# A deeper ring for gathered rows, two fused layer norms, and GpSimd only beside additions out of PSUM

## What is computed

```python
h = _layer_norm(x, ln_in_g, ln_in_b)
z = h @ w_in[i]                                   # pool channels | q | k | v
mix = jnp.concatenate([y_pool, y_attn], axis=-1) @ w_o[i]
h = _layer_norm(DEEPNORM_ALPHA * h + mix, ln1_g[i], ln1_b[i])
ffn = _peer(h, peer_wq[i], peer_subkeys[i], peer_u[i], peer_v[i])
gate = jax.nn.sigmoid(h @ ple_gate_w[i] + ple_gate_b[i])
ple = gate * (p[i] @ ple_w[i])
h = _layer_norm(DEEPNORM_ALPHA * h + ffn + ple, ln2_g[i], ln2_b[i])

# _layer_norm: (x - mean) * rsqrt(var + 1e-5) * g + b, over the 1024 of a token
# _peer: queries = h @ wq; 8 heads each pick 16 of 128 x 128 experts by two sub-keys;
#   a = h . u_tab[expert]; out = sum over picks of softmax * gelu(a) * v_tab[expert]
```

## Time and profile before

| what | us |
|---|---|
| median of 3 runs (1389.04 to 1395.43) | 1389.6 |
| the profiled execution, device time | 1386.17 |
| its span, first to last instruction | 1384.4 |
| PE busy with matmuls | 1329.3 |
| DVE busy | 1159.9 |
| ACT busy | 664.1 |
| POOL busy | 565.8 |
| last matmul of the program ends | 1370.65 |

### The profile page before, as it was taken

The page is one execution under the profiler, slowest core; times in us unless marked ns, Lnnn a source line. Parts: engine busy times, 40 slices in busy tenths (PEclk is TensorE's granted clock), DMA queues, the critical chain, the costliest instruction groups (busy, mean ns, idle before and its releaser), DMA issues.

```text
span 1384.4 us, 23354 instructions
## 1 busy us (share of the span) xinstructions
PE 1329.3 (96%) x7689; PEld 718.7 (52%) x7689; DVE 1159.9 (84%) x2380; ACT 664.1 (48%) x912; POOL 565.8 (41%) x352
## 2 busy tenths in 40 slices
PE   5989899999999999999999999999989999999995
PEld 3554455545665666666655555555534444444442
DVE  6663759999975999999859888888888989988877
ACT  4552545636668767666534333333433434333332
POOL 2640234435555333233326555655564433322202
PEclk9999999999999999999999999999999999999998
DMA  7222132234665999999989999999999999999951
GB/s 302 77 76 92 50 127 83 92 106 148 187 188 174 324 348 366 367 356 356 393 321 377 365 356 369 361 378 355 371 334 389 385 392 390 385 382 371 365 191 62
DMA packets 148654, 384.52 MB, mean 278 GB/s; under 512 B 11761, under 2 KB 71409, under 8 KB 146417
## 3 DMA queue, kind: packets, MB, share of 16 engines
q1 hardware_dynamic: 111728, 249.54, 51.1%
q0 software_dynamic: 36864, 134.23, 25.8%
HBM read 340.74 MB, written 42.99 MB: 277 GB/s over the span
## 4 chain that ended last, share of the span: by engine, by line
PE 76%; DVE 8%; DMA 6%; issue 6%; ACT 2%; DVEq 0%; POOL 0%; SPq 0%; ACTq 0%
PE bank L610 33%; PE bank L599 12%; PE bank L601 11%; PE bank L600 11%; DMA ple_sb<-v_rows_dram,expert_id 4%; PE bank L627 2%; DVE cut L1203 2%; DVE ple_gate L1627 2%; PE bank L814 1%; PE bank L816 1%; PE bank L767 1%; DMA raw<-tiles_dram 1%; PE bank L561 1%; DVE ple_gate L1549 1%; DVE hn L1222 1%
## 5 line engine op out<-in xcount | busy, mean ns | idle before, releaser
L610 PE MATMUL bank<-cut,area 128*128 128x512 f16 x2304 | 504.2, 380 | 8.3 <-DVE area L1615 5.1
L599 PE MATMUL bank<-hT,cut 128*128 128x384 f16 (+1 forms) x1232 | 413.5, 336 | 6.0 <-ACT gelu_out L1080 1.7
L600 PE MATMUL bank<-hT,cut 128*128 128x384 f16 (+1 forms) x1232 | 413.4, 336 | 0.0
L601 PE MATMUL bank<-hT,cut 128*128 128x384 f16 (+1 forms) x1232 | 413.4, 336 | 0.0
L610 PEld LDWEIGHTS bank<-cut,area 128*128 128x128 f16 x2304 | 224.9, 98 | 277.6 <-DVE area L1615 4.6
L875 ACT ACTIVATE cut<-raw 128x1024 f16<-128x1024 f32 x242 | 252.1, 1054 | 212.5 <-PE bank L610 134.8
L1203 DVE SCALAR_TENSOR_TENSOR cut<-raw,cut 128x1024 f16<-128x1024 f32 x242 | 298.0, 1232 | 43.7 <-ACT cut L875 42.7
L548 POOL DMA_INDIRECT ple_sb<-u_rows_dram,expert_id x128 | 200.2, 1564 | 251.8 <-DVE dots_now L1531 243.7
L548 POOL DMA_INDIRECT ple_sb<-v_rows_dram,expert_id x128 | 177.6, 1388 | 244.2 <-DVE ple_gate L1627 233.5
L538 POOL TENSOR_TENSOR cut<-raw,cut 128x1024 f16<-128x1024 f32 x56 | 125.8, 2248 | 159.1 <-ACT cut L885 159.1
L1627 DVE SCALAR_TENSOR_TENSOR ple_gate<-ple_sb,sparse_w_now,ple_gate 128x1024 f32<-128x1024 f32 x128 | 163.8, 1280 | 17.6 <-DMA ple_sb<-v_rows_dram,expert_id 14.8
(11 more groups left out here) (146 smaller groups left out, 1117.6 us busy)
## 6 DMA issues: line engine op xcount, KB each, us to landing
raw<-tiles_dram SPq DMA_DIRECT2D x298, 512.0 KB, 6.4
gates_scratch<-area SPq DMA_DIRECT2D x12, 2048.0 KB, 13.3
area<-gates_scratch SPq DMA_DIRECT2D x32, 768.0 KB, 9.7
gelu_scratch<-gelu_out SPq DMA_DIRECT2D x80, 192.0 KB, 4.9
area<-gelu_scratch SPq DMA_DIRECT2D x20, 768.0 KB, 11.3
norm_rows<-norms_dram SPq DMA_DIRECT2D x3, 1024.0 KB, 8.8
hn<-x_dram SPq DMA_DIRECT2D x4, 512.0 KB, 5.0
ple_sb<-u_rows_dram,expert_id POOLq DMA_INDIRECT x128, 8.4
```

The lines of the kernel that those rows point to most:

```text
L599: nc.tensor.matmul(dst, w[0], hT[:, 0, k, 0:width], start=(k == 0), stop=False)
L600: nc.tensor.matmul(dst, w[0], hT[:, 1, k, 0:width], start=False, stop=False)
L601: last = nc.tensor.matmul(dst, w[1], hT[:, 0, k, 0:width], start=False, stop=(k == KD - 1))
L610: mm = nc.tensor.matmul(bank[:, 2 * tt + h, :], lhs(a)[:, tt * P:(tt + 1) * P], cut[:, t.slot, b, h * HALF:(h + 1) * HALF], start=(first a ...
```

## The change

Four things are edited.

1. **Ring of gathered rows.** ROW_RING goes from 4 to 8. Slots 0 to 3 stay on `ple_sb`, slots 4 and 5 are the two rows of `norm_rows`, slots 6 and 7 the last 2048 columns of `area`. Since the norm rows are overwritten, the third load of `norm_rows` moves on SP's queue from behind the first query tiles to behind the last weight tile and the last addition.
2. **Norm behind attention.** `mix_norm` replaces `row_moments` and `layer_norm`: one DVE instruction makes (x - mean) * weight from two SBUF inputs while ACT takes the root; the Newton step is three small instructions behind the reciprocal's one and needs no shift; ACT multiplies with rstd; POOL adds the bias for tiles 0 to 2; for the last tile DVE makes x * rstd + bias in one. ACT takes the root of the last tile ahead of the first `take_ple`.
3. **First query.** It waits for `ple_out` 7, the second for 8.
4. **Final norm.** Tile 3's steps are laid between the last v tiles' steps. PE runs token tile 2 of the last four v tiles one half after the other. ACT centres and scales tiles 0 and 1; POOL multiplies both with the weight and adds tile 0's bias; DVE adds tile 1's bias as its last instruction and norms tile 2 in halves, which are stored one by one.

```diff
-ROW_RING = 4
+ROW_RING = 8
-POOL_ADDS = ((), (0, 1, 2), (0, 1, 2))
+POOL_ADDS = ((), (0, 1, 2))
-        expert_rows = ple_sb[:, :, :].rearrange("p (s a) n -> p s (a n)", s=ROW_RING)
+        expert_rows = [*(ple_sb[:, 2 * s:2 * s + 2, :].rearrange("p a n -> p (a n)") for s in range(4)),
+                       *(norm_rows[:, s, :] for s in range(2)),
+                       *(area[:, AREA - (s + 1) * D:AREA - s * D] for s in range(2))]
...
+            sp.wait_ge(rows_used, 2 * HK)
+            load_norms(2)
...
-            add_b(2)
+            pool.wait_ge(norms_in, 16 * 3)
+            pool.wait_ge(centred, TT * 2)
+            own.link(nc.gpsimd.tensor_tensor(hn[:, 0, :], hn[:, 0, :], norm_rows[:, 0, :], ALU.mult))
+            nc.gpsimd.tensor_tensor(hn[:, 0, :], hn[:, 0, :], norm_rows[:, 1, :], ALU.add).then_inc(pool_final, 1)
+            pool.wait_ge(centred, TT * 2 + 1)
+            nc.gpsimd.tensor_tensor(hn[:, 1, :], hn[:, 1, :], norm_rows[:, 0, :], ALU.mult).then_inc(pool_final, 1)
...
-            pe.wait_ge(ple_out, 8)
+            pe.wait_ge(ple_out, 7)
...
+                    if isinstance(it, int) and it == 0 and j == 1:
+                        pe.wait_ge(ple_out, 8)
...
+            for h in range(2):
+                for i, t in enumerate(last):
+                    for step, (a, b) in enumerate(((0, 0), (0, 1), (1, 0))):
+                        mm = nc.tensor.matmul(bank[:, 2 * (ND - 1) + h, :],
...
+                mm.then_inc(experts_done, 1)
...
+                own.link(nc.vector.bn_aggr(moments[:, t, :], stats[:, t, :]))
+                nc.vector.tensor_scalar(v, moments[:, t, 1:2], EPS / ALPHA ** 2, None, ALU.add).then_inc(stats_done, 1)
+                dve.wait_ge(norms_in, 16 * 2)
+                own.mark(nc.vector.scalar_tensor_tensor(out=hn[:, t, :], in0=hn[:, t, :], scalar=moments[:, t, 0:1],
+                                                        in1=norm_rows[:, 0, :], op0=ALU.subtract, op1=ALU.mult))
+                dve.wait_ge(rstd_done, norm_batch(1, t) + 1)
+                own.link(nc.vector.reciprocal(r, std[:, t:t + 1]))
+                own.link(nc.vector.tensor_scalar(n, r, r, v, ALU.mult, ALU.mult))
+                own.link(nc.vector.tensor_scalar(n, n, -0.5, 1.5, ALU.mult, ALU.add))
+                nc.vector.tensor_scalar(r, r, n, None, ALU.mult).then_inc(shift_done, 1)
```

More of the change, by code:

```diff
@@ L1185, in late, with final_root, final_normal @@
                         weight_high(N_BOTH + 8 * e + v + 2, (v + 2) % RING, T_LATE + 8 * e + v + 2 - RING)
-                    if end and v == 2:
-                        roots(2, 0)
+                    if end and v == 1:
+                        final_root(0)
+            def final_root(i):
+                t = norm_order(2)[i]
+                act.wait_ge(stats_done, norm_batch(2, i) + 1)
+                nc.scalar.activation(std[:, t:t + 1], variance[:, t:t + 1], ACT.Sqrt).then_inc(rstd_done, 1)
+            def final_normal(i):
+                t = norm_order(2)[i]
+                act.wait_ge(shift_done, norm_batch(2, 0) + i)
+                nc.scalar.activation(hn[:, t, :], hn[:, t, :], ACT.Identity, bias=shift[:, t:t + 1],
+                                     scale=rstd[:, t:t + 1]).then_inc(centred, 1)
             with act.Fori(0, N_LATE // 8 - 1) as e:
@@ L1250, in row_moments @@
+                r, n = rstd[:], newton[:]
+                own.link(nc.vector.reciprocal(r, std[:]))
                 own.link(nc.vector.tensor_tensor(n, r, r, ALU.mult))
-                own.link(nc.vector.tensor_tensor(n, n, variance[:, cols], ALU.mult))
+                own.link(nc.vector.tensor_tensor(n, n, variance[:], ALU.mult))
                 own.link(nc.vector.tensor_scalar(n, n, -0.5, 1.5, ALU.mult, ALU.add))
                 own.link(nc.vector.tensor_tensor(r, r, n, ALU.mult))
-                nc.vector.scalar_tensor_tensor(out=shift[:, cols], in0=moments[:, cols, 0], scalar=-1.0, in1=r,
+                nc.vector.scalar_tensor_tensor(out=shift[:], in0=moments[:, :, 0], scalar=-1.0, in1=r,
@@ L1729, in late @@
                         split_lo(t.plus(SPLIT_AHEAD))
-                    if end and v == 2:
-                        final_rows(0)
-                    if end and v == 4:
-                        layer_norm(2, 0)
             before = own.count
```

209 lines of the change are left out of this document (127 added, 82 removed).

## The result

The changed kernel takes 1372.17 us (median, 1371.36 to 1374.49) where the kernel before takes 1390.56 in the same comparison. The ratio is 0.9865, with a 95% interval of 0.9837 to 0.9892: 18.8 us or 1.35% faster. I had predicted 12.0 us less, 1377.6, and a range down to 1372.0. Direction and places were right, the size was not: the gain is half as large again.

What follows compares the result with a forecast made beforehand. PE was taken as the bound, busy 1329.3 of 1384.4 us, with DVE what it waits for in the touched places. Gains of 2.6 + 6.9 + 2.5 = 12.0 us from the 1389.6 median gave 1377.6 us, range 1372.0 to 1385.5.

Steps and rivals of the forecast that it cites:

- the turning in front: Norm behind attention: PE starts turning tile 2 at 159.2 instead of 161.14 us, 1.9 us won.
- Front: Norm behind attention through first query: 2.6 us gained with DVE held by POOL, 3.5 us without.
- The hold: Norm behind attention: POOL's addition holds DVE's next variance step 0.75 us, making a tile's pitch 5.9 us.
- rival (a): Front and end: POOL does not hold these DVE instructions; 15.1 us gained, 1374.5 us; chance 0.14.
- What is late next: Front: last tile's root at 154.7 us delays `take_ple`; PE's second pair begins near 155.5, ends at 159.1.
- Middle: Stretch 920 to 1035 us: eight slots end DVE's waits for gathered rows and PE's idle time, 6.9 us gained.
- End: Final norm and last v tiles: the span's end comes 2.5 us earlier, 4.7 us if small steps aren't held.
- The 1.27 us: Late v tiles: PE's wait for a low part goes once tile 3's norm is spread; PE ends at 1369.3.
- The base: Whole kernel: the 12.0 us sum, made on the 1386.17 us profiled execution, was subtracted from the 1389.6 us median.
- (b): Middle: full DMA engines mean the deeper ring buys nothing; 5.1 us gained, 1384.5 us; chance 0.14.
- (c): Late v tiles: gathers crowd out weight tiles, costing 18 us; 1395.6 us, slower; chance 0.06.
- (d): Front: its gain does not appear or is lost to a later transfer; 9.4 us gained, 1380.2 us; chance 0.08.

Runs made afterwards that it cites:

- before_look: The kernel before the change, unchanged, profiled a second time: 1390.48 us.
- ring8_alone: The kernel before with only eight ring slots and the norm rows' load moved behind the last addition: 1382.28 us, ratio 0.9937.
- before: The kernel before the change, unchanged, in its first profiled execution: 1386.17 us, span 1384.4 us.
- fill_gap: The kernel before plus three unread products on PE, placed one pair too late, behind the idle piece of the norm behind attention: 1392.19 us, ratio 1.0017.
- front_alone: The kernel before with only the new norm behind attention and the first query waiting for seven instead of eight halves: 1383.78 us, ratio 0.9947.
- after_ring4: The changed kernel with the ring back at four slots: 1378.68 us, ratio to the kernel before 0.9907.
- fill_gap_b: The kernel before plus three unread products on PE inside the idle piece of the norm behind attention: 1387.16 us, ratio 0.9966.
- end_alone: The kernel before with only the new final norm: 1386.43 us, ratio 0.9964.

## Why the prediction was right, and where it failed

Places and mechanisms were right, and the size was too small. The terms that failed are those for PE's idle pieces. The first is the turning in front: the 1.9 us priced for it were 3.5 even at full clock. PE turned tile 2 11.98 us behind the last product with w_o before (161.14 less 149.16) and 8.45 us after (158.06 less 149.61). The second was put at nothing: each piece was priced at its idle time, with the clock taken as 1.00 behind it. In `before_look` the 3.4 us in front cost 2.7 us more by the clock, and the timed runs give the front 7.4 us and not 2.6.

**Front: right places, 2.6 us predicted, 4.6 in the first pair, 7.4 alone.** Three steps of it failed.

- *The hold.* I priced the variance step as held by POOL, since an instruction on 128x4 was the earlier trace rows. The row was right and the step from it wrong: on 128x1 there was no hold in front (0.15 us at 153.00) nor for the Newton steps at the end (0.27 at 1360.35). The pass with two SBUF inputs was held, as I said, but for 0.3 to 0.6 us of each tile, not 0.75. So the mechanism lies between my forecast and rival (a), nearer to (a). Its end of 4.7 us fits; its front of 3.5 is below the 4.6 measured, for the next two reasons.
- *What is late next.* I let `take_ple` wait for the last tile's root until 154.7 and PE's second pair begin near 155.5. The root came at 153.19, `take_ple` at 153.29, and the pair at 154.63. From there PE had no gap at all, so the turning was bound by PE's own order: 1.6 us more than priced for the turning, and 0.4 us more behind it.
- *The clock.* I read 1.00 in the earlier trace rows and took the idle piece at its length. The trace of before could not show it there, but it showed the same thing elsewhere: behind the idle piece of 3.03 us that ends at 101.33 its clock is 0.50 from 102 to 106 us. The Trainium skill, page "TensorE: Matmul & The Clock Gate", section "HAM oscillation — how this bites in real kernels", says that idle gaps of PE between bursts bring the lower clock; the second profile of before agrees (0.50 at 162 to 166), the first does not (1.00 there). I should have had it as a rival: the front by 1.7 to 2.7 us more.

**Middle: the mechanism was right, the remainder was not foreseen.** All of the waits for gathered rows went, as the round of slots said. (One sum on the way was wrong: 1 us per pair over 16.7 pairs is 17 us and not 13, so it did not show DVE falling behind; that the rows held PE is shown by `ring8_alone`.) "So all of it goes" was true of them and not of PE: with the rows there in time, PE waits for the next in line, a weight tile near 1025 us (2.6 us, 1.6 in the second profile) and the gates near 715 us (3.4 and 2.2). The latter I had called untouched by the ring, which it is; but the work arrives earlier at a load whose issue moves less, 707.16 against 709.98 us, so the front gave back some 2 us there. By stretches PE's idle time from 500 to 1045 us fell from 10.7 to 8.3 us in the first pair and from 10.6 to 6.2 in the second, 2.4 to 4.4 and not 6.9. By the timed runs the ring is worth 8.8 alone and 6 in company. The clock falls behind these pieces too: between 1024 and 1048 us it does in five of the seven profiles with four slots (not in `before` and `fill_gap`), and in none of the seven with eight. One stretch each of `front_alone`, `after_ring4`, `fill_gap_b` and `end_alone` (PE only):

```profile
1024.00:1028.00 4.00, 2.15 (x6) 0.74 1.01 374
...
1032.00:1036.00 4.00, 4.00 (x12) 0.57 0.73 254
...
1036.00:1040.00 4.00, 3.54 (x11) 0.66 0.95 322
...
1040.00:1044.00 4.00, 4.00 (x10) 0.50 0.88 306
```

In `before_look` 18 products took 5.74 us there and not the usual 4.06. I take such falls for the larger part of what the timed runs have above the stretches; no run filled these pieces, so the size is argued and not shown.

**End: 2.5 us predicted, 4.4 in the first pair (1.3 and 3.1), 5.0 alone.** The 1.27 us went as laid out, and the norm rows landed in time. The tail was mis-sized by the same hold: the list without it, 4.7 us, was the right one.

**The base.** I subtracted a sum made on one execution from the median of others, 3.4 us above it, as if the change touched none of what lay between. It touched a good part of it: the pieces that it removes are among those behind which the clock falls.

**The rivals.** (b), no gain from the ring, is out: 388 GB/s and more were there, and `ring8_alone` gained. (c), late weight tiles, is out: ACT's wait grew from 58.4 to 72.8 us in the last 300 us, PE's stayed 0. (d), the front lost later, is true for 2 of its 4.6 us.

## What to carry to other kernels

An idle piece of the matrix engine that shows a full clock in one profile may cost nearly double in the next: take two profiles before pricing one, and compare the span and mean clock of every timed run with the profiled one. When one wait is removed, list what arrives earlier at a fixed transfer further on; here moving one load by three places gave back 3 us. A row from the nearest shape is a bound and not a price: a DVE instruction on 128x4 waited for POOL's to end, those on 128x1 did not.

## What the hardware showed that I had not expected

Work that nobody reads made a kernel faster by 4.7 us (2.4 to 7.1); its profile has the clock at 1.00 behind the filled piece. Shortening the idle piece from 3.4 to 0.8 us, or from 3.04 to 1.8, was enough for that in the one profile of each. Behind the same 3.4 us the clock fell in four profiles of kernels with the old norm (0.50 to 0.75 from 162 to 166 us) and stayed at 1.00 in one. DVE's instructions on 128x1 ran beside POOL's two-input additions in their usual 0.15 to 0.28 us, while a pass with two SBUF inputs took 1.83 instead of 1.28 us and ended 1.1 us behind POOL's.
